# Two layers on one core: a new order in the opening's tail, the wide products' heads and the stick-breaking units

## The reference

```python
# opening: per-feature scale and shift from the condition, then the norm of x and ctx
hc = modulate(rmsnorm(ctx, norm_mix[l]), csh_a, csc_a)
hx = modulate(rmsnorm(x, norm_mix[l]), sh_a, sc_a)
...
# first wide product: 1024 x 1024 by 1024 x 5632
a, val = jnp.split(h @ w_up, 2, axis=-1)
a = jax.nn.gelu(dwconv(a, conv_w, conv_b))
return (a * val) @ w_down
...
# stick-breaking attention of the second block, 4 heads of 128
z = jnp.einsum('bhqe,bhke->bhqk', qb, kh) / math.sqrt(E)
log_not = jnp.where(mask, jax.nn.log_sigmoid(-z), 0.0)
excl = lax.cumsum(log_not, axis=3, reverse=True) - log_not
w = jnp.where(mask, jnp.exp(jax.nn.log_sigmoid(z) + excl), 0.0)
return jnp.einsum('bhqk,bhke->bhqe', w, vh)
...
# second wide product, again 1024 x 1024 by 1024 x 5632
gu = hn @ w_up[l]
h = jax.nn.silu(gu[..., :FFN_HIDDEN]) * gu[..., FFN_HIDDEN:]
```

## Time and profile before

| | us |
|---|---|
| median of 3 runs | 3624.54 |
| the runs | 3620.90 to 3627.59 |
| time of the profiled execution | 3622.69 |
| its span, first to last instruction | 3620.8 |

### The profile page before, as it was taken

The page is one execution under the profiler, slowest core; times in us unless marked ns, Lnnn a source line. Parts: engine busy times, 40 slices in busy tenths (PEclk is TensorE's granted clock), DMA queues, the critical chain, the costliest instruction groups (busy, mean ns, idle before and its releaser), DMA issues. The chain is left out here.

```text
span 3620.8 us, 43846 instructions
## 1 busy us (share of the span) xinstructions
PE 3353.2 (93%) x16295; PEld 2679.6 (74%) x16295; DVE 2129.0 (59%) x3010; ACT 1296.4 (36%) x2264; POOL 1289.4 (36%) x1046
## 2 busy tenths in 40 slices
PE   5699999989899999969999999898889979999998
PEld 3577777777688888747888887785557758888886
DVE  5346664454977677885333544574556475555586
ACT  3523343144333334432223333342751233232344
POOL 4021212111655530125445445361525325454111
PEclk7799999989899999989999999879999999999999
DMA  8621112123233337314465343562024423332552
GB/s 254 226 57 52 45 57 97 49 91 119 71 103 107 96 114 267 88 58 139 117 127 125 112 140 128 171 190 64 31 81 146 163 93 102 105 108 93 202 185 96
DMA packets 343340, 422.66 MB, mean 117 GB/s; under 512 B 22006, under 2 KB 249794, under 8 KB 341578
## 3 DMA queue, kind: packets, MB, share of 16 engines
q1 hardware_dynamic: 336008, 396.03, 35.1%
q0 software_dynamic: 6400, 16.94, 1.7%
q10 hardware_dynamic: 722, 6.89, 0.5%
HBM read 296.16 MB, written 122.98 MB: 116 GB/s over the span
## 5 line engine op out<-in xcount | busy, mean ns | idle before, releaser
L2350 POOL TENSOR_TENSOR up_w_lo<-up_w_sum,up_w_hi 128x512 fp32r<-128x512 f32 x176 | 248.4, 1441 | 326.4 <-ACT up_w_hi L2326 324.6
L3368 POOL TENSOR_TENSOR px_w_lo<-px_w_sum,px_w_hi 128x512 fp32r<-128x512 f32 x138 | 195.6, 1447 | 295.2 <-ACT px_w_hi L3179 295.2
L2350 POOL TENSOR_TENSOR up_w_lo<-up_raw,up_w_hi 128x512 fp32r<-128x512 f32 x132 | 201.3, 1541 | 129.3 <-ACT up_w_hi L2326 129.3
L1926 ACT CAST down_hi<-down_room 128x1024 fp32r<-128x1024 f32 x154 | 161.0, 1051 | 210.8 <-PE ps L2206 138.6
L1930 DVE TENSOR_TENSOR down_lo<-down_room,down_hi 128x1024 fp32r<-128x1024 f32 x154 | 190.3, 1240 | 71.9 <-ACT down_hi L1926 70.4
L2326 ACT CAST up_w_hi<-up_w_sum 128x512 fp32r<-128x512 f32 x176 | 99.7, 614 | 323.5 <-DVE up_w_sum L2339 323.5
L768 PE MATMUL ps<-h_hi,stream_hi 128*128 128x512 f32 (+1 forms) x488 | 185.3, 380 | 24.5 <-POOL stream_lo L743 17.2
L2556 PE MATMUL ps<-h_hi_at,up_w_lo 128*128 128x512 f32 x704 | 191.7, 395 | 15.9 <-POOL up_w_lo L2350 15.9
L2556 PE MATMUL ps<-h_hi_at,up_w_hi 128*128 128x512 f32 x704 | 192.9, 396 | 7.2 <-ACT up_w_hi L2326 7.2
L2556 PE MATMUL ps<-h_lo_at,up_w_hi 128*128 128x512 f32 x704 | 191.0, 394 | 0.0
L3179 ACT CAST px_w_hi<-px_w_sum 128x512 fp32r<-128x512 f32 x140 | 79.8, 616 | 306.6 <-DVE px_w_sum L3261 306.6
(11 more groups left out here) (608 smaller groups left out, 8203.1 us busy)
## 6 DMA issues: line engine op xcount, KB each, us to landing
up_raw<-in_w_up SPq DMA_DIRECT2D x88, 512.0 KB, 4.1
down_room<-hid_kept SPq DMA_DIRECT2D x154, 256.0 KB, 2.8
hid_kept<-up_out SPq DMA_DIRECT2D x44, 512.0 KB, 3.6
down_room<-in_w_down SPq DMA_DIRECT2D x88, 256.0 KB, 4.3
px_raw<-in_w_in SPq DMA_DIRECT2D x38, 512.0 KB, 5.2
proj_kept<-xT SPq DMA_DIRECT2D x34, 512.0 KB, 6.0
px_raw<-in_w_gate SPq DMA_DIRECT2D x32, 512.0 KB, 5.2
gates_kept<-xT SPq DMA_DIRECT2D x32, 512.0 KB, 6.0
```

What stands on the lines that cost most here:

```text
L1926: nc.scalar.copy(hi[:, u % R], both(u)).then_inc(hi_made, 1)
L2350: nc.gpsimd.tensor_tensor(w_lo[:, s, :], source(t, i), w_hi[:, s, :].bitcast(F32), ALU.subtract).then_inc(lo_made, 1)
L3368: nc.gpsimd.tensor_tensor(self.w_lo[:, s, :], self.source(t, i), self.w_hi[:, s, :].bitcast(F32), ALU.subtract).then_inc(self.lo_made, 1)
```

## The change

Three places. **Opening:** the x parts of tiles 0 to 5, not only 0 and 1, are modulated ahead of the last turned block; the tiles' ctx parts and roundings are dealt out anew over the four `mod_row` (0, 1 after the first; 2, 3, 4 after the second; 5, 6, 7 after the third; none after the fourth); the rest of tile 7 goes from DVE to POOL; DVE's rests stand ahead of the loop that exhausts `s5dve`.

**Wide products:** `order` puts all of step 0 ahead of the remainder of step 1, with product 6 ahead of 5; ACT casts the seven weights of these places ahead of all `cast_op`; the rests of product 3's operand go from POOL to DVE, between the sums for 4 and for 6; PE waits for one counter, `op_lo`.

**Stick-breaking:** in step u, the lo matmul of u goes behind the logits of u + 2.

```diff
-                for _ in s5dve:
-                    pass
-                for k in (0, 2, 4, 5, 6, 7):
-                    rest(k)
+                for k in (0, 2, 4, 5, 6):
+                    rest(k)
+                for _ in s5dve:
+                    pass
...
-                modulate(0, 0, T, 0)
-                modulate(1, 0, T, 0)
+                for k in range(6):
+                    modulate(k, 0, T, 0)
...
-                        for k in range(4 * (b - NBA) + 2 * i, 4 * (b - NBA) + 2 * i + 2):
-                            if k >= 2:
+                        for k in ((range(0, 2), range(2, 5)), (range(5, 8), range(0)))[b - NBA][i]:
+                            if k >= 6:
                                 modulate(k, 0, T, 0)
...
-                for k in (1, 3):
+                for k in (1, 3, 7):
...
-    order = [(0, 0), (0, 1), (1, 0), (1, 1)] + [(t, i) for t in range(FK) for i in range(2 if t < 2 else 0, N)]
+    order = [(0, 0), (0, 1), (1, 0), (1, 1), (0, 2), (0, 3), (0, 4), (0, 6), (0, 5)] + [(t, i) for t in range(1, FK) for i in range(2 if t < 2 else 0, N)]
...
-                sp.wait_ge(lo_made, place[t, N - 1] + 1)
+                sp.wait_ge(lo_made, max(place[t, N - 2], place[t, N - 1]) + 1)
...
-        cast(act, 1, 0)
-        cast(act, 1, 1)
+        for t, i in order[2:9]:
+            cast(act, t, i)
         cast_op(3, 0)
-        cast(act, 0, 2)
         cast_op(4, 4)
-        for i in range(3, N):
-            cast(act, 0, i)
...
         dve.wait_ge(op_sum, 2 * H)
+        op_rests(3)
         op_sums(6, H, LEFT, high, lambda k: sums[4][:, k])
...
-        for k in range(H):
-            pool.wait_ge(op_hi, k + 1)
-            pool.wait_ge(op_sum, H + k + 1)
-            nc.gpsimd.tensor_tensor(ops[3][1][:, k], sums[3][:, k], ops[3][0][:, k].bitcast(F32), ALU.subtract).then_inc(op_lo_pool, 1)
-        for t, i in order[4:]:
+        for t, i in order[2:]:
             rest(pool, t, i)
...
-                    pe.wait_ge(op_hi, OP_AT[i] + H)
-                    if i == 3:
-                        pe.wait_ge(op_lo_pool, H)
-                    else:
-                        pe.wait_ge(op_lo, LO_AT[i] + H)
+                    pe.wait_ge(op_lo, OP_AT[i] + H)
...
+
+            def sums_end(u):
+                q0 = units[u][3]
+                R = c.ps[:, 4 + u % 2, :]
                 pe.wait_ge(lo_ready, u + 1)
...
                 if u + 2 < N:
                     logits(u + 2)
+                if u < N:
+                    sums_end(u)
```

More of the change, by code:

```diff
@@ L2265, in seven_products @@
     raw_loaded = [[c.sem(f"{name}_raw{s}{part}") for part in range(2)] for s in range(2)]
-    OP_AT, LO_AT = {3: 0, 4: H, 6: 2 * H, 5: 3 * H}, {4: 0, 6: H, 5: 2 * H}
-    op_hi, op_lo, op_lo_pool, op_sum, shift_made, s_made, hi_made, lo_made, used, p1_copied, u_made, tap_made, conv_made, act_made, out_made = (
-        c.sem(f"{name}_{n}") for n in ("op_hi", "op_lo", "op_lo_pool", "op_sum", "shift", "s", "hi", "lo", "used", "p1", "u", "tap", "conv", "act", "out"))
+    OP_AT = {3: 0, 4: H, 6: 2 * H, 5: 3 * H}
+    op_hi, op_lo, op_sum, shift_made, s_made, hi_made, lo_made, used, p1_copied, u_made, tap_made, conv_made, act_made, out_made = (
+        c.sem(f"{name}_{n}") for n in ("op_hi", "op_lo", "op_sum", "shift", "s", "hi", "lo", "used", "p1", "u", "tap", "conv", "act", "out"))
     def quarter(t, part, half):
@@ L2524, in gpsimd @@
     def gpsimd(pool):
-        for t, i in order[2:4]:
-            rest(pool, t, i)
-        for k in range(H):
-            pool.wait_ge(op_hi, k + 1)
-            pool.wait_ge(op_sum, H + k + 1)
-            nc.gpsimd.tensor_tensor(ops[3][1][:, k], sums[3][:, k], ops[3][0][:, k].bitcast(F32), ALU.subtract).then_inc(op_lo_pool, 1)
-        for t, i in order[4:]:
+        for t, i in order[2:]:
             rest(pool, t, i)
```

## The result

| | before | after |
|---|---|---|
| median of 4 runs each, us | 3622.72 | 3596.60 |
| the runs | 3615.50 to 3627.59 | 3595.16 to 3599.62 |
| ratio, 95% interval | | 0.9931 [0.9916, 0.9946] |
| span of the profiled execution | 3620.8 | 3596.1 |
| its mean granted clock | 0.953 | 0.956 |

The changed kernel is faster by 26.1 us where 20 were forecast; by the interval of the ratio the gain lies between 19.6 and 30.4 us. The median is at the low end of the range of 3597 to 3613, 0.4 us past it. Of the four terms the opening's held, the units' was 1.7 us too small, the first head's far too small and the second head's too large, and 4 to 5 us have no place in any edit.

What follows compares the result with a forecast made beforehand. PE was taken as the bound, full in the wide products past their heads. Gains of 14.0 (units), 1.5 (opening), 0.5 and 4.2 (heads), together 20.2 us, gave 3602.5 profiled and a 3604.3 us median; range 3597 to 3613.

Steps and rivals of the forecast that it cites:

- What bounds the kernel: Whole kernel: PE is full in the wide products past their heads, so time won in the three places stays won.
- Units: Stick-breaking stage: GpSimd's lo and the lo matmul leave the loop, PE becomes the bound; gain 14.0 us, 10.7 to 16.
- Opening: End of the opening: mainly one rest less on DVE, x parts fitting in ACT's idle time; gain 1.5 us, 0 to 4.5.
- Rival C: Clock stays up in opening and first head, DVE isn't held: +3 opening, +1.5 first head, +2 units; 3597 us; chance 0.13.
- Head 1: Head of the first wide product: (1, 4) starts earlier, less a low-clock charge; gain 0.5 us, -1 to 2.
- DVE's sequence up to there is 1.5 us earlier, and 0.3 more: First head: DVE's take that (1, 4) needs done at 952.6 instead of 954.43, so (1, 4) starts 1.8 us earlier.
- I take 1.3 us for the product: First head: 1.3 us charged to (1, 4) for slow groups after PE has stood for 2.7 us.
- Head 2: Head of the second wide product: PE gets to (1, 4) earlier, without a wait; gain 4.2 us, 2.5 to 5.
- B: Stick-breaking stage: DVE's args and soft wait behind the later lo; units gain only 6, whole 12, 3612 us; chance 0.17.
- D: Wide products' heads: later product 3 and low clock after longer stops; heads -1 instead of +4.7, 3610 us; chance 0.07.
- E: Stick-breaking stage: the loop over the running sums becomes the bound; slower, 3636 us; chance 0.02.
- F: All three places: the change does nothing where it says; chance 0.01.

Runs made afterwards that it cites:

- the repeat: The changed kernel run again with nothing changed: 3597.04 us.
- the opening alone: The kernel before with only the opening's part of the change, run twice: 3617.41 us (ratio 0.9980) and 3616.26 us.
- the same experiment as for B: Against the changed kernel, the lo matmul of unit u put further back, behind rest_of_block of u - 1 and values of u - 2: 3596.61 us.

## Why the prediction was right, and where it wasn't

**What bounds the kernel: right.** Won time stayed won: from (1, 4) on PE is full in both products. From there to the last matmul of the product it takes 388.7 to 388.9 us in the first and 388.7 to 389.2 us in the second, in all twelve traces, however long the head was.

**Units: 14.0 forecast, 15.7 measured** (15.5 in the repeat). The mechanism was right in each point: lo's wait gone, PE the bound at 5.28 us for two wide units (5.30 forecast), 1.27 gained from 384 to 512 (1.34), 0.81 from 256 to 384 (0.8). PE's wait is 1.8 us where under 4 was forecast. The mis-sized terms, by the 24 pairs of lo starts: the eight wide steps give 8.3 us instead of 6.6, since the first two of each run of wide units take 4.8 and 5.0 us rather than 5.3 (in the first PE still multiplies the narrower units' values; why the second is short is not shown); the narrow steps, seven and not the eight of the prediction since 24 pairs have 23 steps between them, give 0.1 instead of -1.2 (six lose 0.07 to 0.16 each, the first, from 128 to 256, gains 0.8); and lo of the very first unit comes 1.0 us later, which the sum didn't have. 8.3 + 5.1 + 3.2 + 0.1 - 1.0 = 15.7.

**Opening: 1.5 forecast, 1.4 measured** (38.43 and 38.45 for 39.81 and 39.98: 1.4 to 1.6). Each row came: 1.92 us left of ACT's 7.01, one rest less on DVE, the short instruction held by GpSimd's rest, PE's stop shorter by 0.75 us (3.18 for 3.93; 0.7 forecast). The starts that the prediction named are some 0.8 us too late since the last turned block came 0.9 us earlier in this run (141.30 for 142.19). Rival C fell here: behind the stop of 3.18 us PE's groups still took their long time, as they did before.

**Head 1: 0.5 forecast, 2.7 measured**, the same in five traces of the new order (54.16 to 54.22). DVE's loop begins 1.4 us earlier (1.5 forecast). Two steps failed. First, "DVE's sequence up to there is 1.5 us earlier, and 0.3 more": it was 1.3 more. The wait for product 6 inside the loop, 0.44 us, is gone, and the first tap takes 1.53 us instead of 2.27. GpSimd is at work beside it in both kernels. GpSimd's instruction of that time, after and before:

```profile
942.87 1.28 POOL L2350 TENSOR_TENSOR up_w_lo<-up_w_sum,up_w_hi 128x512 fp32r<-128x512 f32 x1
...
949.23 1.28 POOL L2350 TENSOR_TENSOR up_w_lo<-up_w_sum,up_w_hi 128x512 fp32r<-128x512 f32 x1
```

It ends at 944.15 and at 950.51, and the tap ends 1.09 us later both times (945.24 and 951.60). After the change the tap begins only 0.44 us ahead of GpSimd's end, before 1.18 us: how GpSimd's row of instructions happens to lie against DVE's decides it. Second, "I take 1.3 us for the product": a charge for a low clock behind a long stop. The stop is there but in two parts, 1.58 us for ACT and 0.58 us for DVE, and behind both the groups take 1.20 us, full clock. The repeat shows how little the clock decides here. The same kernel, second execution:

```profile
932.18 1.20 PE L2544 MATMUL ps<-up_t_hi,up_w_hi 128*128 128x512 f32 x4 [2.05 <-DVE up_t_lo L2464]
933.22 1.82 PE L2544 MATMUL ps<-up_t_lo,up_w_hi 128*128 128x512 f32 x4
...
942.73 1.20 PE L2544 MATMUL ps<-h_hi_at,up_w_hi 128*128 128x512 f32 x4 [0.48 <-ACT up_p L2427]
...
946.34 1.19 PE L2544 MATMUL ps<-up_t_hi,up_w_hi 128*128 128x512 f32 x4 [0.58 <-DVE up_a L2490]
...
2969.21 1.20 PE L2544 MATMUL ps<-h_hi_at,up_w_hi 128*128 128x512 f32 x4 [2.35 <-ACT up_p L2427]
...
2972.07 1.07 PE L2544 MATMUL ps<-up_t_hi,up_w_hi 128*128 128x512 f32 x4
```

At 933.22 the clock falls where in the first execution it stayed up; PE loses 1.1 us more on its way to (1, 3), waits 1.1 us less for ACT (0.48 for 1.58), and (1, 4) comes at 54.20 us instead of 54.17. Low-clock time ahead of such a wait is free. In the old order it wasn't: in the two runs of the opening alone DVE's take of product 6, which stood behind product 5, waited 1.61 and 1.55 us for a slow PE (0.44 in the kernel before), and head 1 took 58.1 us instead of 56.8. With product 6 ahead of 5 DVE had no such wait, in the repeat with its low clock either.

**Head 2: 4.2 forecast, 1.2 measured** (3.7 in the repeat). This is the step that failed: "PE gets to (1, 4) at about 2993.4, 4.2 us earlier and without a wait". Without a wait for DVE, yes; but the sum let (1, 3) run directly behind (1, 2) and never asked who reads the bank that (1, 3) takes. The rule was in the prediction's hands: it was used for (1, 4) alone. So was the instruction: the last of the earlier trace rows has DVE's take at 2994.01 waiting 0.88 us for the same copy of ACT. ACT's copy ends 49.27 us into the stage (2966.68 less 2917.41), so (1, 3) can't start before, and its product of 2.7 us at full clock puts (1, 4) at 52.1 or later; the forecast had 50.7. What comes on top is the clock, and here, behind the last wait, it counts: behind 2.38 us it fell (the rows of the second head above, 1.91 us for the second group) and (1, 4) came at 53.79, behind 2.35 us in the repeat it didn't and (1, 4) came at 52.19. Over five traces of each order the heads last 55.4 us on average before (54.97 to 55.96) and 53.1 after (52.19 to 53.79): 2.3 us gained. With ACT's copy moved the gain is 5.8 against the mean, more than the 4.2 forecast.

**The sum.** By the first pair of traces 15.7 + 1.4 + 2.7 + 1.2 = 21.0 us against 20.2 forecast, so the terms' errors nearly cancel: +1.7, -0.1, +2.2, -3.0. The medians differ by 26.1 us, the spans by 24.7. The 4 to 5 us between are in stretches without an edit, and no larger than what the same kernel varies by (in this pair of traces they are 5.4 us of the span, less the 1.7 us that the low clock took at the end): the four runs of the kernel before spread over 12.1 us, and 21.0 lies within the 19.6 to 30.4 us of the interval. The prediction gave them nothing, and it couldn't have. That the total came out near the forecast, with one head mis-sized each way, is luck in the sum.

**The rivals.** B (DVE's order takes over) shows in the rows as it was described, DVE waiting for lo, but costs nothing. C was right on the time and wrong on the reason: the opening's clock didn't stay up, and in the first head the clock made no difference to the end. D fell: both heads gain. For E the same experiment as for B decides. F fell, since each place gives its part alone. The Trainium skill ("SBUF — State Buffer", who interferes with whom) has DVE blocked for the whole of GpSimd's instruction; that is what the 0.21 us instruction shows (held 0.82 us, free again when GpSimd's rest ended), and the tap that ended 1.09 us behind GpSimd's instruction fits it too. For two long rows side by side it gives somewhat too much: beside GpSimd's, DVE's sums of product 3 began 1.70 us apart in the changed kernel, while 0.61 alone and 1.28 for GpSimd's add up to 1.89. These sums, for which the prediction wanted 1.7 us each, took 5.76 us for four: 0.68 for the first, which GpSimd didn't hold up, and 1.75 to 1.78 for the others.

## To carry to other kernels

When work is moved ahead on the engine that sets the end, list for each of its next products every reader of the buffer it takes, and look where that reader's instruction stands in its own engine's order: a wait that was hidden by 1 us becomes the last one. A low clock costs where someone waits for PE; ahead of a wait of PE for another engine it only shortens that wait. And judge a change of 1 to 3 us by the pieces between landmarks next to the edit: in repeats of one kernel they came out within 0.3 us in the units and 0.1 us in the first head, while the whole moved by 4 to 10 us for no edit. Even a piece can move by 1 us without an edit in it, when the clock at its start is another.

## What the runs showed of the hardware

- Stops of the same length were followed by either clock. Behind 2.38 us the second group took 1.91 us (1.2 GHz) and behind 2.35 us 1.08 us (2.4 GHz), in two runs of one kernel; behind 2.04 and 2.05 us it took 1.09 and 1.82 us; behind 2.49 us the granted clock of the next 5 us was 0.66 and 1.00. The clock behind a stop of 2.0 to 2.5 us could not be told from its length here.
- DVE's tap, begun during an instruction of GpSimd, ended 1.09 us after that instruction did, whether it had begun 0.44 or 1.18 us before its end.
- Stretches of 150 to 180 us with many waits between engines varied by up to 4.0 us from run to run of the same kernel, while the units repeated within 0.3 us.
- A large wait of DVE, 21.7 us in a stage of 118 us, cost nothing beside a full PE.
